# Cache copies in packets of 4088 bytes in place of 32704 and 16352

## The reference

```python
k_all = jnp.concatenate([k_buf, k], axis=1)
keep = max(0, k_all.shape[1] - MAX_WINDOW)
new_state = (k_all[:, keep:], v_all[:, keep:], ...)
```

## Time and profile before

| | |
|---|---|
| profiled execution | 2130.82 us |
| its span, first to last instruction | 2129.0 us |
| median of three executions | 2130.69 us (2120.62 to 2135.42) |
| TensorE busy | 2029.7 us, 95% |
| VectorE, POOL, ScalarE busy | 1481.9, 781.4, 744.1 us |
| granted TensorE clock, mean | 0.978 |
| moved by DMA | 683.04 MB, mean 321 GB/s |
| read from and written to memory | 618.78 MB and 196.32 MB |

### The profile page before, as it was taken

One profiled execution on the slowest core, in us unless ns is written; L12 is line 12 of the kernel. 1 busy time (PEld: TensorE's weight loads), 2 busy tenths in 40 slices (PEclk: granted clock), 3 DMA queues, 4 the chain that ended last, 5 costly groups with the idle time before them and its releaser, 6 DMA issues.

```text
span 2129.0 us, 33458 instructions
## 1 busy us (share of the span) xinstructions
PE 2029.7 (95%) x12130; PEld 1687.5 (79%) x12130; DVE 1481.9 (70%) x3108; ACT 744.1 (35%) x1112; POOL 781.4 (37%) x483
## 2 busy tenths in 40 slices
PE   7998999998889999899999999999989999999998
PEld 7998975555453348899999999999977877777776
DVE  1375125554573335579889699999788889888988
ACT  2232113444341002124343355555433333333332
POOL 4342310000110003247889732222365555555630
PEclk9999999999989999999999999999999999999999
DMA  9998877787998579837999878887999999999993
GB/s 328 341 307 319 311 279 300 315 354 253 339 329 331 162 262 352 312 124 269 346 362 356 312 279 306 300 306 279 382 401 389 392 392 392 392 386 387 386 363 138
DMA packets 202351, 683.04 MB, mean 321 GB/s; under 512 B 18305, under 2 KB 84225, under 8 KB 194177
## 3 DMA queue, kind: packets, MB, share of 16 engines
q1 hardware_dynamic: 150256, 442.42, 57.6%
q0 software_dynamic: 46080, 167.79, 20.6%
q10 hardware_dynamic: 5904, 71.39, 9.7%
HBM read 618.78 MB, written 196.32 MB: 383 GB/s over the span
## 4 chain that ended last, share of the span: by engine, by line
PE 56%; DMA 21%; issue 9%; DVE 8%; POOL 3%; ACT 2%; SPq 0%; POOLq 0%; DVEq 0%; ACTq 0%
DMA overlay<-peer_v 16%; PE bank L188 11%; PE bank L189 10%; PE bank L190 10%; PE bank L1474 5%; PE bank L2076 4%; POOL overlay L363 3%; DVE overlay L2288 2%; PE bank L666 2%; DVE arena L2089 2%; PE bank L682 2%; DMA overlay<-peer_wq 2%; DMA overlay<-peer_u 1%; PE bank L732 1%; ACT overlay L2196 1%
## 5 line engine op out<-in xcount | busy, mean ns | idle before, releaser
L188 PE MATMUL bank<-overlay 128*128 128x384 f32 (+4 forms) x2768 | 943.7, 341 | 37.5 <-DVE overlay L2294 18.9
L189 PE MATMUL bank<-overlay 128*128 128x384 f32 (+4 forms) x2768 | 928.5, 335 | 0.0
L190 PE MATMUL bank<-overlay 128*128 128x384 f32 (+4 forms) x2768 | 927.8, 335 | 0.0
L188 PEld LDWEIGHTS bank<-overlay 128*128 128x128 f32 (+1 forms) x2768 | 522.6, 189 | 86.6 <-issue 36.4
L190 PEld LDWEIGHTS bank<-overlay 128*128 128x128 f32 (+1 forms) x2768 | 522.0, 189 | 31.4
L189 PEld LDWEIGHTS bank<-overlay 128*128 128x128 f32 (+1 forms) x2768 | 522.7, 189 | 30.1
L1913 POOL DMA_INDIRECT arena<-peer_v,arena x160 | 258.0, 1613 | 226.5 <-DVE arena L2089 213.1
L1634 POOL TENSOR_TENSOR overlay<-overlay 128x1024 fp32r<-128x1024 f32 x86 | 206.7, 2404 | 291.9 <-ACT overlay L1627 288.3
L2089 DVE SCALAR_TENSOR_TENSOR arena<-arena 128x1024 f32<-128x1024 f32 x160 | 205.3, 1283 | 0.1
L1627 ACT CAST overlay<-overlay 128x1024 fp32r<-128x1024 f32 x144 | 150.1, 1044 | 157.5 <-DMA overlay<-peer_u 87.1
L1913 POOL DMA_INDIRECT arena<-peer_rows,arena x80 | 109.9, 1373 | 243.4 <-DVE arena L2084 223.8
(11 more groups left out here) (239 smaller groups left out, 2176.4 us busy)
## 6 DMA issues: line engine op xcount, KB each, us to landing
overlay<-peer_u SPq DMA_DIRECT2D x128, 512.0 KB, 7.9
overlay<-peer_v SPq DMA_DIRECT2D x128, 512.0 KB, 11.7
o_vsall<-cache_vall SPq DMA_DIRECT2D x22, 2044.0 KB, 27.2
o_ks<-cache_k ACTq DMA_DIRECT2D x10, 4088.0 KB, 17.9
arena<-cache_kT SPq DMA_DIRECT2D x32, 896.0 KB, 11.2
arena<-cache_v SPq DMA_DIRECT2D x56, 512.0 KB, 6.6
arena<-w_out SPq DMA_DIRECT2D x48, 512.0 KB, 5.6
act<-arena SPq DMA_DIRECT2D x128, 192.0 KB, 8.4
```

Source lines behind the costliest of these rows:

```text
L188: pe.matmul(out, lhs[0], rhs[0], start=start, stop=False)
L189: pe.matmul(out, lhs[0], rhs[1], start=False, stop=False)
L190: return pe.matmul(out, lhs[1], rhs[0], start=False, stop=stop)
```

## The change

Both kinds of copy get packets of 1022 floats, 4088 bytes. A full copy then has 128 pieces x 8 sequences, 1024 packets, 64 per DMA engine; a half copy 64 x 8, 512 packets, 32 per engine. The regions, the number of DMAs, the queues, their order and the waits are the same.

```diff
--- before.py
+++ after.py
@@ -267,7 +267,7 @@
 
         copied = sem("copied")
         CHUNK = (WIN - NT) * D // 16
-        PIECE = CHUNK // 16
+        PIECE = CHUNK // 128
 
         def copy_cache(eng, side, x):
 
@@ -279,7 +279,7 @@
         def copy_half(eng, y):
 
             cutout = lambda ap, lo: ap.rearrange("b s d -> b (s d)")[:, bass.ds(y * (CHUNK // 2) + lo, CHUNK // 2)]\
-                .rearrange("b (s n) -> s b n", n=PIECE // 2)
+                .rearrange("b (s n) -> s b n", n=PIECE)
             eng.dma_start(cutout(t["o_vsall"], 0), cutout(t["cache_vall"], NT * D)).then_inc(copied, 16)
```

## The result

The changed kernel is much slower. It took 3022.99 us, median of four executions (3006.07 to 3026.66); the kernel before, run beside it, 2133.06 us (2120.62 to 2141.67, four executions). The ratio is 1.4176, 95% interval 1.4112 to 1.4239. The forecast, 2123 us in a range of 2109 to 2143, was wrong in sign and size. The profiled execution took 3026.66 us, 896 more than the one before.

The account below looks back on a forecast made before the run. TensorE was taken to set the projection's pace, DMA close behind, with weight loads slowed by copies. Terms -10.2 - 0.6 + 2.8 = -8.0 us took the profiled 2130.82 to 2123 us, range 2109 to 2143.

Parts of the forecast that it names:

- The rate of the copies: Where loads queue behind copies on SP's queue, copies were to take 3% more time: +2.8 us.
- bad end: Worst case for copies that loads queue behind: 289 GB/s, 11% more time, a loss of 10.3 us.
- The splitting rule: For all copies, unaligned 4088-byte packets need 17 pieces, not 16: about 6% longer, sum 3 us worse.
- Rival 2: Projection and SP-queued stages: small copies much slower in memory, 250 GB/s, total 2186 us; range 2133 to 2190, chance 0.17.
- 93 us of copy time: Copy time that loads queue behind: 31 us (510 to 541) plus about 80% of 78 us (808 to 886).
- Issue: On SP and ACT, longer copy-issue stalls were to be covered, SP's by its 79.6 us wait: cost nothing.
- a reserve of about 10: On ACT, casts behind copies were to absorb 5 to 8 us stalls; otherwise up to 5 us per group.
- with its queue full meanwhile: Query stage: a stalled SP issues `peer_wq` later, but the load keeps its place in the queue; no cost.
- Turns between q10 and q1: Input projection: `w_in` packets wait for shorter copy packets, so blocks land in some 10 us, not 20.2.
- The stop at 188 us: End of the projection's feature blocks: TensorE's stop for late weights was to go, gaining 10.2 us.
- Rival 1: Projection: `w_in` loads still land in about 20 us, only the rate term stays; 2129 to 2135 us, chance 0.18.
- Rival 3: All copies: shorter packets bring copies nearer the rate of loads; 2103 to 2117 us, chance 0.15.

Follow-up runs that it names:

- experiment 9: Kernel before with all copies cut to 4032-byte packets every 4096 bytes, at multiples of 64 bytes, some bytes left out: 2130.84 us.
- 10: As experiment 9, but writes alone moved on by 8 bytes: 2551.04 us.
- experiment 17: Changed kernel's packet count, with 4032-byte packets every 4064 bytes, at multiples of 32 bytes, 1.4% of bytes left out: 2290.91 us.
- experiment 18: As experiment 17, but reads and writes both moved on by 8 bytes: 2684.93 us.
- experiment 15: As experiment 9, but SP's six full copies issued sequence by sequence in 48 DMAs, without the 8 MB jump after each packet: 2117.03 us.
- 14: As experiment 9, but writes and reads both moved on by 8 bytes: 2572.57 us.
- experiment 6: Kernel before with copies in 4608- and 2304-byte packets, reads moved on by 8 bytes, writes at aligned starts: 2245.39 us.
- experiment 8: Kernel before with only the full copies cut into 4672-byte packets at multiples of 64 bytes: 2163.7 us, ratio 1.0181.
- experiment 16: Kernel before with full copies in 16352-byte packets, half copies unchanged: 2132.44 us, ratio 1.002.
- experiment 5: Changed kernel with the last 64 bytes of each packet left out, a gap between packets: 3004.98 us.
- experiment 4: Kernel before with all copies in 8176-byte packets at multiples of 16 bytes: 2524.69 us.

## Why the prediction was wrong

**The rate of the copies: the step that failed.** Taken as 3% more time with a bad end of 11%, measured 320/110 = 2.9 times. The bad end came from a row of 16 KB copies, at multiples of 32 bytes, the good end from loads; neither the 8 sequences' jump after each 4 KB nor a ragged write was in any of them, and I called 8-byte starts "a little". Two prices, each shown alone, make up most of the fall: ragged writes (234 to 163, experiments 9 and 10; 237 to 139, 17 and 18) and the jump (312 to 234, 15 and 9). Worked out per packet, 4032 bytes by a sixteenth of the rate: 207 ns clean without the jump, 276 with it, 396 and 464 ragged, and 595 for the change's 4088. The last 130 to 200 ns are open. These are means. The trace keeps the time of each packet: of the change's 32768 copy packets half take 227 ns or less, while the 15% that take over 1 us make up half of the time; in experiment 17 such packets are 2%. So the price comes as a few long waits and not as a toll on each packet.

The splitting rule of the Trainium skill, "DMA: Bandwidth & Descriptors", section "How a descriptor splits into AXI transactions", had given 6% for unaligned 4088-byte packets, by the 17 fetches in place of 16. That 6% no run tests. In experiments 10 and 14 a packet moved by 8 bytes needs 16 fetches by this rule as before, its slots lying 4096 bytes apart, and in experiment 6 most packets started off the 256-byte boundaries already. There the reads cost next to nothing (163 and 156 GB/s; 250 against 231 to 279). The writes, moved by the same 8 bytes, cost 30% of the rate, for which the rule has no term. The row of the Trainium skill, same page, on 4 and 8 MiB pitches ("Latency and other measured facts") I set aside because the long packets showed nothing of it. At 4 KB the runs agree with it in direction: the jump takes a quarter of the rate, not half, in the one clean pair of runs. No run changed the pitch itself.

**The arithmetic around the rate held, for the projection.** Rival 2 has a group cost 2.1/389 + 6.3/r. With r = 110 that is 5.4 + 57.3 = 62.7 us, against 24.1 now: ten groups lose 386 us. Measured: 385.0, with stalls and slow clock in it. So close a match is partly luck: the window itself moved 129 GB/s, loads and copies together, which makes 65 us a group. So rival 2 had the mechanism's place and one of its two causes, and priced it at 250 GB/s where 110 came.

**What lies behind SP's copies was mis-sized.** I counted 93 us of copy time that loads wait for. SP carries 6 full copies of 4.19 MB and 22 halves of 2.09, 71.1 MB, 222 us at 320 and 646 at 110: 424 more. The time beyond 93 us, that of the six full copies above all, was covered by SSD work while they took some 80 us (25.1 MB at 320); at 230 us it isn't, hence the 175.7 us for `w_out`. Of the 500 us lost there, up to 424 are explained so. The rest is open; a lower clock has a part in it where TensorE works between waits: the median matmul of L1683 takes 421 ns in place of 275. In SSD it has hardly any: the granted clock, 0.52 while TensorE stood idle from 930 to 1017, was 0.94 from 1017 to 1110.

**Issue: costed at nothing, wrong.** A stall of 5 to 8 us was to fit into a reserve of about 10. It measured up to 73.3 us for the half copies on ACT in the change, median 39.4, and up to 21.9 in experiment 8, where packets were clean. On SP the 79.6 us of waiting were to cover the issue of the full copies; with the half behind them it took 255. Even in experiment 16, with twice the packets in the full copies, TensorE waits 13.8 us behind SP's stalls. The premise that "with its queue full meanwhile" a load keeps its place overlooked that the work behind a stall is not only loads of that queue: on ACT it is casts.

**Turns between q10 and q1: right in kind, where copies are clean.** Forecast about 10 us to land; 10.9 in experiment 9 (9.3 to 12.3), 11.9 in 8, against 20.2. The stop at 188 us goes in experiments 8 and 16, as forecast for -10.2. But in experiment 16 the median landing is 19.6, where the model gives 12 to 14; and in the change it is 36.6, with 7 loads in the window in place of 20:

```profile
L300 SPq DMA_DIRECT2D overlay<-w_in x7: 332/333/333, 61.1 to 121.1; - x7
...
DMA to landing us min/median/max: 31.3/36.6/41.1
```

Turns alone, 8 x 0.6 us above a lone load, would make 8 to 12. So one packet of q1 does not wait for just one of q10 when those are slow; what it waits for is not known. Rival 1 ("loads stay slow") fell with the clean packets of 4 KB; in experiment 16 the loads did stay slow, so something of its kind may be at work there; no run tests that. Rival 3 (faster copies) fell with every run: no window of the six full copies was above 320.

**Left open.** What in the memory makes ragged writes slow: the bytes read and written that the page counts are those of the kernel before (618.78 and 196.32 MB), so extra reads, if there are any, do not show there. The step from 139 (18) and 156 (14) GB/s to the 110 of the change; a part of it is that the DMA engines stood idle at times, share 0.91 there and 0.82 in experiment 5, against 1.04 in 18. The low rate of experiment 4. A complete copy in short clean packets without the jump, which may gain landing time and keep 312 GB/s, was not run; no kernel that moves all bytes beat the one before.

## What to carry to other kernels

A bound from rows holds only for what those rows share: before shortening packets, ask what the new packet has that no row has (the alignment of its two ends, the distance to the next packet), and let the bad end be far when there is something. In a copy of short packets keep both ends of every write at multiples of 32 bytes, and order it so that an engine's next packet lies beside its last. When packets multiply, look at what stands behind the issuing instruction on its engine, and redo the sum of cover at the slower rate: transfers that were hidden come out one after another.

## What the runs showed of the hardware beyond that

In this copy from memory to memory the place of the writes within 32 bytes sets the rate of short packets, and that of the reads hardly matters: 4032-byte packets, 234 GB/s clean, 227 with writes 32 bytes on, 161 and 163 with them 16 and 8 on, 156 with the reads moved too. At 32 KB a start moved on by 8 takes 320 to 313. Two neighbours that share a block of memory have no part in it: 95 GB/s with a gap of 64 bytes between them, 110 without. The DMA engines show a share of 1.01 at 312 GB/s (experiment 15) and of 1.04 at 139 (experiment 18), so a busy share says nothing of the rate.
